# Bias and running maximum of the neighbourhood and dilated attention scores in one VectorE instruction per 128 queries

## The chip, the cores and the metric

The kernel runs on one core of one Trainium2 chip. The metric is the device time of one execution in microseconds. All tensors are fp32. A weight matrix is split into a rounded part and a rest, both in the format that TensorE multiplies fast, so each weight chunk passes through ScalarE (the rounded part, `W_hi`) and VectorE (the rest, `W_lo`) before TensorE can use it.

## The reference, cut to what matters

The model is a chain of blocks over 256 tokens of width 1024. Two of its attention stages are touched by the change: neighbourhood attention (8 heads of width 64, each query sees a window of 8 by 16 grid cells and adds a learned bias) and dilated attention (16 heads of width 64, three groups of keys at strides 1, 4 and 16, masked).

```python
# neighbourhood attention, one row of the grid
sc = einsum('bchd,bicjhd->bhcij', q_row, k_win) * dh ** -0.5
sc = sc + bias
p = softmax(sc)
return einsum('bhcij,bicjhd->bchd', p, v_win)
...
# dilated attention, one block of 128 queries, per group g of keys
sc = einsum('bqhd,bqjhd->bhqj', q_blk[:, :, g], k_sel) * dh ** -0.5
sc = where(valid, sc, -1e30)
m = max(sc); e = exp(sc - m); z = sum(e)
o = einsum('bhqj,bqjhd->bqhd', e / z, v_sel)     # groups are then merged by a softmax over m + log z
```

## The kernel before

All work of a core is written out per engine, in one fixed order, and the engines meet only in semaphores. A list of stages (`make_plan`) is walked by each engine's program. Between the attention stages lie projections and MLPs, in which TensorE streams weight chunks of 1 MB.

An attention stage (kind `attend`) goes by units. In the stages called `even` (8 neighbourhood heads `na`, then 8 latent-attention heads `mla`) and `dilated` (16 heads `dil`) a unit is a pair of heads; I call its first head a and its second head b. `even` has units 0 to 3 with `na` heads and 4 to 7 with `mla` heads; `dilated` has units 0 to 7. A head's scores lie in PSUM, as 256 queries in two halves of 128 (`t` = 0, 1) by 256 keys (`na`) or 512 keys (`dil`: 256 of stride 1, 128 each of the two others).

For each head:

- `scores(u)` on TensorE (L707) writes the scores of both heads of unit u to PSUM. It first waits until the heads that had the same banks have been read. For heads with a bias that is the semaphore `s_read`.
- `soft(n)` on VectorE adds bias or mask and finds the maximum: for `dil` one SCALAR_TENSOR_TENSOR over 128x1024 (L1211), for `na` two over 128x256 (L1219), which scale the score, add, write the sum to SBUF and raise `s_read`; then a wait for `s_read`, and one TENSOR_REDUCE (L1244) that writes the negated maximum to `e["mx"]` and raises `s_soft`.
- `exps(n)` on ScalarE (L1022) waits for `s_soft`, makes two exponentials, each with its row sum.
- `normalise(n)` on VectorE waits for both, then one RECIPROCAL (L1249) and two TENSOR_SCALAR (L1252).
- `transposes(n)` on TensorE (L725) waits for it; `keep_pt(n)` on ScalarE (L1032) copies the transposes to SBUF.
- `values(u)` on TensorE (L742, and L751 for `dil`) multiplies by the values; `output(u)` on VectorE (L1264) copies the result out.

The order within a stage is fixed by these loops. In `dilated`, TensorE goes `scores(u+1)`, `transposes` of a and b of unit u, `values(u)`; VectorE goes `normalise` a and b of u, `output(u-1)`, `soft` a and b of u+1; ScalarE goes `keep_pt` a and b of u, `exps` a and b of u+1. In `even`, scores are made two units ahead, and so is `soft`. The `soft` of the very first unit is called from within the projection in front of the stage (`open_attention`), ahead of the copy of that projection's last block (L1410 for `dilated`, L1391 for `even`); `scores` of the next unit waits for that copy. The stage behind `dilated` is the output projection `od_o`, whose first matmul is at L624.

Of the kernel before, what the change touches and what calls it, by code (L numbers as in the profile page):

```python
# [23 lines left out]
ALU = mybir.AluOpType  # L24
# [4 lines left out]
S = 256  # L29
# [5 lines left out]
EPS = 1e-6  # L35
NEG = -1e30
NA_H, NA_W = 8, 512
DIL_G, DIL_H = 3, 16
# [4 lines left out]
SLOTS = 6  # L43
# [72 lines left out]
def make_plan(w):  # L116
# [24 lines left out]
    p.add("mla_in", "mla_in")  # L141
    up("na_qk", w["ev_w_in"], 0, 1, post="copy", dest="na_qk", latents=True)
    up("na_qk", w["ev_w_in"], 256, 1, post="copy", dest="na_qk", at=512)
    p.add("mla_turn", "mla_turn")
# [54 lines left out]
def build_program(nc, a, out):  # L199
# [18 lines left out]
    with ctx:  # L218
# [109 lines left out]
        def head(what, h):  # L328
            if what == "na":
                pb = 64 * (h % 2)  # L330
                q = region(R["na_qk"] + (h // 2) * S, S)[pb:pb + 64, :]
                k = region(R["na_qk"] + (4 + h // 2) * S, S)[pb:pb + 64, :]
                v = lambda g, kt: region(R["na_v"] + kt * 512 + h * 64, 64)
                y = H0 + (h // 2) * S
                return dict(G=1, q=[q], k=[k], v=v, y_at=y, pb=pb, scale=64 ** -0.5, bias="na", R=R, h=h)
            if what == "mla":
# [6 lines left out]
            if what == "dil":  # L343
                pb, blk, pair = 64 * (h % 2), h // 8, h // 2
                q = [region(DIL0 + g * DIL_SIZE + pair * S, S)[pb:pb + 64, :] for g in range(3)]
                k = [region(DIL0 + g * DIL_SIZE + 2048 + pair * S, S)[pb:pb + 64, :] for g in range(3)]
                v = lambda g, kt: region(DIL0 + g * DIL_SIZE + 4096 + blk * 1024 + kt * 512
                                         + (h % 8) * 64, 64)
                y = H0 + pair * S
                return dict(G=3, q=q, k=k, v=v, y_at=y, pb=pb, scale=64 ** -0.5, bias="dil", R=RD, h=h)  # L350
            if what == "fox":
# [62 lines left out]
        for n, e in enumerate(heads):  # L414
# [16 lines left out]
            e["read"] = n_read  # L431
            n_read += bool(e["bias"])
            at = e["R"]["sm"]
# [147 lines left out]
        def _(pe):  # L581
# [110 lines left out]
            def scores(u):  # L692

                both = [heads[n] for n in units[u]]
                for e in both:
                    for prev in e["score_prev"]:
                        if heads[prev]["bias"]:
                            pe.wait_ge(s_read, heads[prev]["read"] + 1)
                        else:
                            pe.wait_ge(s_exp, 2 * prev + 2)  # L700
# [244 lines left out]
        def _(act):  # L945
# [14 lines left out]

            def cross(g, u, pair):

                act.wait_ge(chunk_done, g + 1)
                if not isinstance(u, int) or u >= 2:
                    act.wait_ge(acc_read, u - 1)
                A(T0[:, pair, :].rearrange("p (f t) -> p f t", f=2),  # L966
                  PS[:, 2 * pair:2 * pair + 2, S:2 * S], ACT.Copy).then_inc(cross_out, 1)

# [48 lines left out]
            def exps(n):  # L1017
                e = heads[n]
                act.wait_ge(s_soft, n + 1)
                for t in range(TT):  # L1020
                    src = e["probs"] if e["bias"] else e["scores"]
                    A(e["probs"][:, e["cols"][t]], src[:, e["cols"][t]], ACT.Exp,  # L1022
                      bias=e["mx"][:, t:t + 1], scale=1.0 if e["bias"] else e["scale"],
                      accum_out=e["z"][:, t:t + 1]).then_inc(s_exp, 1)
# [13 lines left out]
            for st in stages:  # L1038
# [17 lines left out]
                elif kind in ("up", "conv", "natural"):  # L1056
                    def body(i, ss=(0, 1)):
                        for s in ss:
# [8 lines left out]
                            if kind != "natural":  # L1067
                                cross(g0 + 2 * i + s, u0 + 2 * i + s, pairs[s])
                            if st.get("dest") == "latent" and s == 0:
# [89 lines left out]
        def _(dve):  # L1159
# [19 lines left out]
            def add_halves(st, dst, u, pair):  # L1179


                dve.wait_ge(cross_out, u - st["u"] + st["cross0"] + 1)
                return V.tensor_tensor(dst.rearrange("p (f t) -> p f t", f=2),  # L1183
                                       PS[:, 2 * pair:2 * pair + 2, 0:S],
# [12 lines left out]
            def soft(n):  # L1197
# [7 lines left out]
                if e["bias"] is None:  # L1205
# [3 lines left out]
                    return  # L1209
                if e["bias"] == "dil":  # L1210
                    V.scalar_tensor_tensor(e["probs"], e["scores"], e["scale"],  # L1211
                                           const("dil"), ALU.mult, ALU.add
                                           ).then_inc(s_read, 1)
                elif e["bias"] == "na":
                    if e["h"] == 0:
                        dve.wait_ge(bias_ready, 1)
                    for t in range(TT):
                        at = R["na_bias"] + e["h"] * SLOTS * GRID + (2 - 2 * t) * GRID
                        last = V.scalar_tensor_tensor(pr[:, t, :], sc[:, t, :], e["scale"],  # L1219
                                                      region(at, S), ALU.mult, ALU.add)  # L1220
                    last.then_inc(s_read, 1)
                else:
# [18 lines left out]
                    last.then_inc(s_soft, 1)  # L1241
                    return
                dve.wait_ge(s_read, e["read"] + 1)
                V.tensor_reduce(e["mx"], pr, AXIS.X, ALU.max, negate=True).then_inc(s_soft, 1)  # L1244

# [479 lines left out]
```

## Time and profile before

| | |
|---|---|
| median of 3 runs | 1936.98 us (1935.32 to 1937.48) |
| the profiled execution | 1936.47 us, of which the span from first to last instruction 1934.7 us |
| TensorE busy | 1848.3 us, 96% |
| VectorE busy | 1209.9 us, 63% |
| ScalarE busy | 935.0 us, 48% |
| mean granted TensorE clock | 0.987 |

The busy shares are averages over stages with different limits. The two attention stages that the change touches run from about 79 to 123 us (`even`) and from 554 to 627 us (`dilated`) after the span's start. Everything in the text below is told in us after that start.

### The profile page before, as it was taken

How to read it: one execution, taken by the hardware profiler on the slowest of the kernel's cores; microseconds unless marked ns; L12 is line 12 of the kernel's file. 1: busy time of each engine (PE TensorE's matmuls, PEld its weight loads, DVE VectorE, ACT ScalarE, POOL GpSimd, SP SyncE). 2: the span in 40 equal slices, each digit the busy share in tenths (PEclk: the TensorE clock that was granted, in tenths of full speed). 3: DMA queues.
4: the chain of work that ended last, by engine and by line, in shares of the span. 5: the costliest groups of instructions: out<-in, count | busy, mean ns of one | idle time of the engine just before them, and what ended most of it. 6: DMA issues, size and time to landing. Idle time of an engine off the chain costs nothing.

```text
span 1934.7 us, 27716 instructions
## 1 busy us (share of the span) xinstructions
PE 1848.3 (96%) x9804; PEld 1558.3 (81%) x9804; DVE 1209.9 (63%) x1436; ACT 935.0 (48%) x1384; POOL 271.9 (14%) x219
## 2 busy tenths in 40 slices
PE   8789999999997999999999999999999999989998
PEld 7668887777776888888888878888888888778886
DVE  6866655666778666466556656564646556756554
ACT  6354445333346544455545446454545445545443
POOL 2110021212200101210011940002000011020012
PEclk9899999999999999999999999999999999999999
DMA  5525654454430565555555535555535555245553
GB/s 186 178 69 162 184 194 174 173 173 154 163 120 1 173 187 191 190 161 194 192 177 190 180 131 184 185 194 182 187 110 195 179 191 185 98 141 173 177 192 130
DMA packets 214812, 319.32 MB, mean 165 GB/s; under 512 B 5984, under 2 KB 167008, under 8 KB 214496
## 3 DMA queue, kind: packets, MB, share of 16 engines
q1 hardware_dynamic: 213616, 313.45, 48.7%
q0 software_dynamic: 848, 4.85, 0.7%
q8 instruction: 37, 0.61, 0.1%
q10 hardware_dynamic: 288, 0.23, 0.0%
q14 instruction: 23, 0.19, 0.0%
HBM read 317.46 MB, written 1.05 MB: 165 GB/s over the span
## 4 chain that ended last, share of the span: by engine, by line
PE 82%; DVE 11%; issue 3%; ACT 2%; DMA 1%; POOL 1%; DVEq 0%; ACTq 0%; POOLq 0%
PE PS L619 24%; PE PS L617 12%; PE PS L624 12%; PE PS L626 12%; PE PS L625 12%; DVE W_lo L1172 5%; PE PS L613 4%; PE PS L614 2%; PE PS L707 1%; PE PS L689 1%; PE PS L725 1%; DMA W_raw<-in_mem_w_kv 1%; DVE U L1420 1%; PE PS L742 1%; ACT U L1022 0%
## 5 line engine op out<-in xcount | busy, mean ns | idle before, releaser
L1172 DVE TENSOR_TENSOR W_lo<-W_raw,W_hi 128x1024 fp32r<-128x1024 f32 x598 | 772.7, 1333 | 291.9 <-ACT W_hi L953 290.7
L619 PE MATMUL PS<-XN,W_hi 128*128 128x512 f32 x2072 | 739.5, 396 | 0.0
L953 ACT ACTIVATE W_hi<-W_raw 128x1024 fp32r<-128x1024 f32 x598 | 598.1, 1050 | 183.2 <-PE PS L626 168.6
L617 PE MATMUL PS<-XN,W_lo 128*128 128x256 f32 x2072 | 579.0, 279 | 0.0
L619 PEld LDWEIGHTS PS<-XN,W_hi 128*128 128x128 f32 x2072 | 389.2, 188 | 80.0
L617 PEld LDWEIGHTS PS<-XN,W_lo 128*128 128x128 f32 x2072 | 391.1, 189 | 13.9
L1603 POOL TENSOR_TENSOR SX<-U,SX 128x512 fp32r<-128x512 f32 (+1 forms) x98 | 128.5, 1316 | 1334.0 <-ACT SX L1015 1334.0
L624 PE MATMUL PS<-W_hi,SX 128*128 128x512 f32 x780 | 303.9, 390 | 1.4 <-issue 1.3
L626 PE MATMUL PS<-W_hi,SX 128*128 128x512 f32 x780 | 303.1, 389 | 0.0
L625 PE MATMUL PS<-W_lo,SX 128*128 128x512 f32 x780 | 303.1, 389 | 0.0
L966 ACT ACTIVATE T<-PS 128x512 f32<-128x512 f32 x152 | 90.9, 598 | 437.9 <-PE PS L619 437.9
L1183 DVE TENSOR_TENSOR T<-PS,T 128x512 f32<-128x512 f32 x128 | 88.4, 691 | 244.4 <-ACT T L966 244.4
L1015 ACT ACTIVATE SX<-U 128x512 fp32r (+2 forms) x98 | 60.5, 629 | 231.7 <-PE PS L626 231.7
L624 PEld LDWEIGHTS PS<-W_hi,SX 128*128 128x128 f32 x780 | 146.4, 188 | 32.4 <-issue 2.5
L626 PEld LDWEIGHTS PS<-W_hi,SX 128*128 128x128 f32 x780 | 146.4, 188 | 30.3
L625 PEld LDWEIGHTS PS<-W_lo,SX 128*128 128x128 f32 x780 | 146.4, 188 | 30.2
L624 PE MATMUL PS<-W_hi,XN 128*128 128x512 f32 (+2 forms) x368 | 144.4, 392 | 13.8 <-DVE W_lo L1172 13.2
L625 PE MATMUL PS<-W_lo,XN 128*128 128x512 f32 (+2 forms) x368 | 141.7, 385 | 0.0
L626 PE MATMUL PS<-W_hi,XN 128*128 128x512 f32 (+2 forms) x368 | 141.4, 384 | 0.0
L613 PE MATMUL PS<-XN,W_hi 128*128 128x512 f32 x296 | 118.8, 402 | 8.3 <-DVE W_lo L1172 7.5
L624 PEld LDWEIGHTS PS<-W_hi,XN 128*128 128x128 f32 x368 | 70.2, 191 | 32.1 <-DVE W_lo L1172 18.2
L614 PE MATMUL PS<-XN,W_lo 128*128 128x256 f32 x296 | 82.3, 278 | 0.0
(144 smaller groups left out, 1526.6 us busy)
## 6 DMA issues: line engine op xcount, KB each, us to landing
W_raw<-in_ffn_w_gate_up SPq DMA_DIRECT2D x88, 1024.0 KB, 5.1
W_raw<-in_mlp_w SPq DMA_DIRECT2D x64, 1024.0 KB, 5.2
W_raw<-in_ffn_w_down SPq DMA_DIRECT2D x44, 1024.0 KB, 4.9
W_raw<-in_od_w_in SPq DMA_DIRECT2D x36, 1024.0 KB, 4.9
W_raw<-in_a_w_in SPq DMA_DIRECT2D x14, 1024.0 KB, 5.0
W_raw<-in_mem_w_kv SPq DMA_DIRECT2D x8, 1024.0 KB, 5.2
W_raw<-in_w_kvf SPq DMA_DIRECT2D x8, 1024.0 KB, 5.4
W_raw<-in_ev_w_in SPq DMA_DIRECT2D x6, 1024.0 KB, 5.8
```

Source lines behind the costliest of these rows:

```text
L613: mm(bank, wT(W_hi, slot, k, fb), both, start=True, stop=False)
L614: mm(bank[:, S:], wT(W_lo, slot, k, fb), xn[:, k, 0, :], start=False, stop=False)
L617: mm(bank[:, S:], wT(W_lo, slot, k, fb), xn[:, k, 0, :], start=False, stop=False)
L619: last = mm(bank, wT(W_hi, slot, k, fb), both, start=False, stop=k == KD - 1)
L624: mm(bank, xh, wh, start=start, stop=False)
L625: mm(bank, xh, wl, start=False, stop=False)
L626: return mm(bank, xl, wh, start=False, stop=stop)
L953: A(W_hi[:, slot, halves(h)], W_raw[:, slot, halves(h)], ACT.Copy).then_inc(w_hi, 1)
L966: A(T0[:, pair, :].rearrange("p (f t) -> p f t", f=2), PS[:, 2 * pair:2 * pair + 2, S:2 * S], ACT.Copy).then_inc(cross_out, 1)
L1172: V.tensor_tensor(W_lo[:, slot, halves(h)], W_raw[:, slot, halves(h)], W_hi[:, slot, halves(h)], ALU.subtract).then_inc(w_lo, 1)
L1183: return V.tensor_tensor(dst.rearrange("p (f t) -> p f t", f=2), PS[:, 2 * pair:2 * pair + 2, 0:S], T0[:, pair, :].rearrange("p (f t) -> p ...
L1603: nc.gpsimd.tensor_tensor(SX[:, slot, 1, 0:st["ks"] * S], down_src(st, j), SX[:, slot, 0, 0:st["ks"] * S], ALU.subtract).then_inc(st_lo, 1)
```

## The change

`soft` for `na` and `dil` heads becomes two calls of `tensor_tensor_reduce`, one for each half of 128 queries: out = (score + bias) times a factor of `-masked`, and the running minimum of what was written, starting from 3e38, goes to `e["mx"]`. What is written is thus negated and the minimum is the negated maximum. The exponential then has a scale of -1. The instruction has only one factor, on the sum; for the masks (0 or -1e30) that factor may be the score's scale, and for the `na` bias it may not, so q is scaled by 1/8 where it leaves its projection (`times`): on ScalarE as a scale of a copy that is there already, on VectorE as SCALAR_TENSOR_TENSOR in place of TENSOR_TENSOR (2 instructions). `s_read` is no longer raised for these heads. TensorE's `scores` waits for `s_soft` of the heads that had the banks.

```diff
-    up("na_qk", w["ev_w_in"], 0, 1, post="copy", dest="na_qk", latents=True)
-    up("na_qk", w["ev_w_in"], 256, 1, post="copy", dest="na_qk", at=512)
+    up("na_qk", w["ev_w_in"], 0, 1, post="copy", dest="na_qk", latents=True, times=64 ** -0.5)
+    up("na_qk", w["ev_w_in"], 256, 1, post="copy", dest="na_qk", at=512, times=64 ** -0.5)
...
-                        if heads[prev]["bias"]:
+                        if heads[prev]["bias"] == "fox":
                             pe.wait_ge(s_read, heads[prev]["read"] + 1)
+                        elif heads[prev]["bias"]:
+                            pe.wait_ge(s_soft, prev + 1)
...
-                  PS[:, 2 * pair:2 * pair + 2, S:2 * S], ACT.Copy).then_inc(cross_out, 1)
+                  PS[:, 2 * pair:2 * pair + 2, S:2 * S], ACT.Copy, scale=times).then_inc(cross_out, 1)
...
-                      bias=e["mx"][:, t:t + 1], scale=1.0 if e["bias"] else e["scale"],
+                      bias=e["mx"][:, t:t + 1], scale={None: e["scale"], "fox": 1.0}.get(e["bias"], -1.0),
...
+                if st.get("times"):
+                    return V.scalar_tensor_tensor(dst.rearrange("p (f t) -> p f t", f=2),
+                                                  PS[:, 2 * pair:2 * pair + 2, 0:S], st["times"],
+                                                  T0[:, pair, :].rearrange("p (f t) -> p f t", f=2),
+                                                  ALU.mult, ALU.add)
...
-                if e["bias"] == "dil":
-                    V.scalar_tensor_tensor(e["probs"], e["scores"], e["scale"],
-                                           const("dil"), ALU.mult, ALU.add
-                                           ).then_inc(s_read, 1)
-                elif e["bias"] == "na":
-                    if e["h"] == 0:
+                if e["bias"] in ("na", "dil"):
+                    if (e["bias"], e["h"]) == ("na", 0):
                         dve.wait_ge(bias_ready, 1)
                     for t in range(TT):
-                        at = R["na_bias"] + e["h"] * SLOTS * GRID + (2 - 2 * t) * GRID
-                        last = V.scalar_tensor_tensor(pr[:, t, :], sc[:, t, :], e["scale"],
-                                                      region(at, S), ALU.mult, ALU.add)
-                    last.then_inc(s_read, 1)
+                        if e["bias"] == "na":
+                            add = region(R["na_bias"] + (e["h"] * SLOTS + 2 - 2 * t) * GRID, S)
+                        else:
+                            add = const("dil")[:, t * 2 * S:(t + 1) * 2 * S]
+
+                        last = V.tensor_tensor_reduce(
+                            out=pr[:, t, :], in0=sc[:, t, :], in1=add, scale=-e["masked"], scalar=FAR,
+                            op0=ALU.add, op1=ALU.min, accum_out=e["mx"][:, t:t + 1])
+                    last.then_inc(s_soft, 1)
...
-                    return
-                dve.wait_ge(s_read, e["read"] + 1)
-                V.tensor_reduce(e["mx"], pr, AXIS.X, ALU.max, negate=True).then_inc(s_soft, 1)
```

On VectorE, the turn from one unit of `dilated` to the next (the end of `normalise`, `output`, then `soft` of heads a and b) stood like this before. U, T and K are the SBUF tensors of scores and mask, ST holds the statistics.

```order
L1264 COPY U<-PS 128x4x64 [waits s_pv]
L1211 SCALAR_TENSOR_TENSOR U<-PS,K 128x1024 [waits s_pt,s_score]
L1244 TENSOR_REDUCE ST<-U 128x2 [waits s_read]
L1211 SCALAR_TENSOR_TENSOR U<-PS,K 128x1024 [waits s_pt,s_score]
L1244 TENSOR_REDUCE ST<-U 128x2 [waits s_read]
L1249 RECIPROCAL ST<-ST 128x2 [waits s_exp]
```

And after the change. Each call is emitted as two instructions: the pass over the scores, and one that writes out the running value.

```order
L1270 COPY U<-PS 128x4x64 [waits s_pv]
L1227 ISA U,ST<-PS,K 128x512 [waits s_pt,s_score]
L1227 ISA ST 128x1
L1227 ISA U,ST<-PS,K 128x512
L1227 ISA ST 128x1
L1227 ISA U,ST<-PS,K 128x512 [waits s_pt,s_score]
L1227 ISA ST 128x1
L1227 ISA U,ST<-PS,K 128x512
L1227 ISA ST 128x1
L1255 RECIPROCAL ST<-ST 128x2 [waits s_exp]
```

Four instructions became eight, of which four are of one element per partition, and the wait between sum and maximum is gone. On TensorE nothing moves; the start of `scores` in the same place waited like this before:

```order
L751 MATMUL PS<-U 64x128 x7
L707 MATMUL PS<-U 128x256 [waits s_read]
L707 MATMUL PS<-U 128x256
L707 MATMUL PS<-U 128x128 x4
L707 MATMUL PS<-U 128x256 x2
```

and waits like this after:

```order
L754 MATMUL PS<-U 64x128 x7
L710 MATMUL PS<-U 128x256 [waits s_soft]
L710 MATMUL PS<-U 128x256
L710 MATMUL PS<-U 128x128 x4
L710 MATMUL PS<-U 128x256 x2
```

The semaphore that frees the score banks is now the one raised at the end of `soft`, not the one raised when the scores had been read.

## Rows read from the trace of the kernel before

**Rows 1.** Windows of the dilated stage: length, busy of PE, PEld, DVE, ACT, POOL, PEclk
```profile
561.70:563.60 1.90, 0.01 (x2) 0.01 (x2) 1.90 (x3) 1.16 (x3) 0.00 (x0) 1.00 0.22 91
563.60:566.10 2.50, 2.50 (x24) 2.16 (x24) 1.84 (x6) 0.36 (x2) 0.00 (x0) 0.75 0.00 0
...
617.00:619.80 2.80, 0.02 (x1) 0.02 (x1) 2.65 (x5) 1.93 (x7) 0.00 (x0) 0.94 0.00 0
619.80:627.00 7.20, 7.00 (x41) 5.35 (x41) 1.57 (x4) 5.66 (x10) 2.75 (x2) 0.55 0.00 0
```

**Rows 2.** Timeline of one dilated unit: start, duration, engine, line, operation, [idle before <-releaser]
```profile
582.26 1.23 DVE L1211 SCALAR_TENSOR_TENSOR T<-PS,K 128x1024 f32<-128x1024 f32 x1
...
584.67 1.21 DVE L1211 SCALAR_TENSOR_TENSOR T<-PS,K 128x1024 f32<-128x1024 f32 x1
585.92 1.22 DVE L1244 TENSOR_REDUCE ST<-T 128x2 f32<-128x1024 f32 x1
...
586.14 2.03 PE L707 MATMUL PS<-U 64*128 64x256 f32 x24 [0.79 <-DVE T L1211]
...
587.17 0.72 ACT L1022 ACTIVATE T<-T,ST 128x512 f32<-128x512 f32 x1 [0.86 <-DVE ST L1244]
...
588.72 0.17 DVE L1249 RECIPROCAL ST<-ST 128x2 f32<-128x2 f32 x1 [0.60 <-ACT T L1022]
...
590.18 1.22 DVE L1211 SCALAR_TENSOR_TENSOR U<-PS,K 128x1024 f32<-128x1024 f32 x1
```

**Rows 3.** Timeline of TensorE from the dilated stage's third `scores` to its fourth
```profile
571.44 2.03 PE L707 MATMUL PS<-U 64*128 64x256 f32 x24
...
574.83 1.07 PE L725 MATMUL PS<-K,T 128*128 128x128 f32 x8 [0.34 <-ACT U L1032]
...
576.23 1.08 PE L742 MATMUL PS<-U 128*64 128x256 f32 x8 [0.34 <-ACT U L1032]
...
578.24 2.03 PE L707 MATMUL PS<-U 64*128 64x256 f32 x24
```

**Rows 4.** Timeline at the dilated stage's opening and end
```profile
562.32 1.21 DVE L1410 COPY U<-PS 128x1024 f32<-128x1024 f32 x1
...
563.59 2.61 PE L707 MATMUL PS<-U 64*128 64x256 f32 x24 [1.92 <-DVE U L1410]
...
620.10 0.19 ACT L1022 ACTIVATION_READ_ACCUMULATOR T<-T,ST 128x1 f32 x1
...
626.91 0.50 PE L624 MATMUL PS<-W_hi,SX 128*128 128x512 f32 x1
```

**Rows 5.** Groups of VectorE by form: count, busy us, mean ns of one, idle before
```profile
L1219 DVE SCALAR_TENSOR_TENSOR U<-PS,U 128x256 f32<-128x256 f32 x16 | 6.0, 415 | 2.0 <-PE PS L707 2.0
L1234 DVE SCALAR_TENSOR_TENSOR U<-U,ST,K 128x256 f32<-128x256 f32 x8 | 3.8, 479 | 0.0
```

**Rows 6.** Timeline of VectorE at the first `mla` unit of `even`
```profile
103.09 0.68 DVE L1206 TENSOR_REDUCE ST<-PS 128x2 f32<-128x512 f32 x1
...
103.81 0.17 DVE L1207 TENSOR_SCALAR ST<-ST 128x2 f32<-128x2 f32 x1
103.89 0.69 DVE L1206 TENSOR_REDUCE ST<-PS 128x2 f32<-128x512 f32 x1
```

**Rows 7.** Timeline of the `na` units of `even`, `soft` of unit 1 first
```profile
85.21 0.75 DVE L1219 SCALAR_TENSOR_TENSOR U<-PS,U 128x256 f32<-128x256 f32 x2
...
88.93 1.94 PE L725 MATMUL PS<-K,U 128*128 128x128 f32 x8 [4.90 <-DVE U L1252]
...
92.93 0.76 DVE L1219 SCALAR_TENSOR_TENSOR U<-PS,U 128x256 f32<-128x256 f32 x2 [1.97 <-PE PS L707]
...
95.82 0.51 ACT L1022 ACTIVATE U<-U,ST 128x256 f32<-128x256 f32 x1 [0.29 <-DVE ST L1244]
...
98.01 0.74 DVE L1219 SCALAR_TENSOR_TENSOR U<-PS,U 128x256 f32<-128x256 f32 x2
```

**Rows 8.** Window at the end of `even`, columns as in rows 1
```profile
117.10:118.90 1.80, 0.00 (x0) 0.03 (x1) 1.67 (x6) 1.80 (x7) 0.00 (x0) 1.00 0.00 0
```

More of the change, by code:

```diff
@@ L36 @@
 NEG = -1e30
+FAR = 3e38
 NA_H, NA_W = 8, 512
@@ L334, in head @@
                 y = H0 + (h // 2) * S
-                return dict(G=1, q=[q], k=[k], v=v, y_at=y, pb=pb, scale=64 ** -0.5, bias="na", R=R, h=h)
+                return dict(G=1, q=[q], k=[k], v=v, y_at=y, pb=pb, scale=64 ** -0.5, masked=1.0, bias="na", R=R, h=h)
             if what == "mla":
@@ L349, in head @@
                 y = H0 + pair * S
-                return dict(G=3, q=q, k=k, v=v, y_at=y, pb=pb, scale=64 ** -0.5, bias="dil", R=RD, h=h)
+                return dict(G=3, q=q, k=k, v=v, y_at=y, pb=pb, scale=64 ** -0.5, masked=64 ** -0.5, bias="dil", R=RD, h=h)
             if what == "fox":
@@ L431, in build_program @@
             e["read"] = n_read
-            n_read += bool(e["bias"])
+            n_read += e["bias"] == "fox"
             at = e["R"]["sm"]
@@ L959, in ahead, with cross @@
                     split_hi(g + 1, 1 - slot)
-            def cross(g, u, pair):
+            def cross(g, u, pair, times=1.0):
                 act.wait_ge(chunk_done, g + 1)
@@ L1067, in body @@
                             if kind != "natural":
-                                cross(g0 + 2 * i + s, u0 + 2 * i + s, pairs[s])
+                                cross(g0 + 2 * i + s, u0 + 2 * i + s, pairs[s], st.get("times", 1.0))
                             if st.get("dest") == "latent" and s == 0:
```

## The prediction

> **What bounds the kernel now.** TensorE is busy 96% of the span, but that is an average over stages, so I went to the places where the changed lines run. The busy groups of VectorE say where: L1211, L1219 and their L1244 run only in `even` (about 79 to 123) and `dilated` (554 to 627). I then read the chain of waits there, the timeline to see what each engine waits for, and last the granted clock.
>
> In `dilated` the middle units are a ring through VectorE and ScalarE [rows 2]. `soft` of head a starts at 582.26, that of head b at 584.67, its maximum at 585.92, and the exponentials of b can start at 587.17: 4.9 us of `soft`. They take 1.55 (587.17 to 588.72, where RECIPROCAL had waited 0.60 for them). From there, normalising b and the copy of the output take 1.46 to the next `soft` at 590.18. Sum 7.92, and that is the period: 590.18 - 582.26. TensorE waits in it: its `scores` at 586.14 had been idle 0.79 for head b's sum (L1211).
>
> TensorE has a shorter ring of its own. From the third `scores` to the fourth, 571.44 to 578.24, it takes 6.80 [rows 3]: transposes of b start 3.39 in, `values` 1.40 later, and two short waits of 0.34 for ScalarE's copies are part of it. So a unit costs 7.9 where VectorE sets the pace and 6.8 where TensorE does, and the trace of before has one of each kind.
>
> Both ends of the stage wait for VectorE too. At the opening, the copy L1410 starts at 562.32, behind `soft`, though TensorE has stood still since 561.67 (it starts at 563.59 after 1.92 idle) [rows 4]. TensorE's clock, still 1.00 while it stands, is 0.75 in the next 2.5 us [rows 1]. At the end TensorE does next to nothing for 2.8 us, and the 7.2 after it run at 0.55, close to the lower level of 1.2 GHz [rows 1].
>
> In `even` the `na` units have the same ring: 92.93 to 98.01 is 5.08, the next, to 103.09, again 5.08 [rows 6, 7]. `soft` takes 2.89 until b's exponentials start at 95.82, and 2.19 follow. In front of the first transposes at 88.93 TensorE had been idle 4.90, and what released it was VectorE's normalisation, which stands behind `soft` of unit 1 from 85.21 on.
>
> **The price of the new instruction.** The trace has none of its kind. A head of `dil` now takes two passes of 128x512 and two short instructions that write out one value; I call pass and write-out together c, and c' for the 128x256 of `na`. Lower bound: an instruction over 128x512 takes 0.69, one over two values 0.17, and the next one starts 0.08 after such a short one's start [rows 6], so the last 0.08 or so of each lie under its successor. That is 0.61 + 0.08 = 0.69 for c. A 128x256 takes 0.415 [rows 5], two of them 0.75 [rows 7]: 0.34 + 0.08 = 0.42 for c'. Upper bound for a pass at the ordinary rate: nothing overlaps, 0.69 + 0.17 = 0.86 and 0.415 + 0.17 = 0.59. I take 0.75 and 0.46, nearer to the lower ends, since the short instruction in rows 6 overlaps on both sides. `soft` of both heads is then 4c = 3.0 instead of 4.9 in `dilated`, and 4c' = 1.84 instead of 2.8 in `even`.
>
> The Trainium skill (Vector Engine (DVE) Microarchitecture Reference, Measured stream behaviour on trn2) gives built-in operations and programs of several micro-operations alike 1.04 ns per column and some 75 ns per instruction. By that page c would be an estimated 0.68; the sum would stay the same, as will be seen, since 6.8 is then set by TensorE.
>
> **Even, -2.5.** The first `soft` pair (at 81) lies under TensorE's projection: nothing. That of unit 1 is in front of the first transposes: 88.93 comes 0.9 earlier (2.77 of `soft` to 1.84). The two rings behind it become 0.05 + 2c' (head a) + 1.13 (a's exponentials) + 2.19 = 4.3, since b's exponentials now wait for a's and not for b's maximum: 0.8 less each. The `mla` units are unchanged. 0.9 + 1.6 = 2.5.
>
> **Dilated, opening, -0.6.** `soft` of unit 0 from 557.55 on now ends at about 560.6. The copy L1410 starts when the last chunk is done, 561.7, lasts 1.21, and TensorE starts at 563.0 instead of 563.59.
>
> **First unit, -1.0.** From 563.59 to 571.44 are 7.85, of which a part is the fallen clock. TensorE's idle time in front becomes 1.3 us instead of 1.92. I take the clock as staying up, as it does at the end of `even`, where TensorE stands still for 1.8 us at 1.00 [rows 8]. The unit then costs 6.8.
>
> **Middle units, -4.5.** The unit of rows 3 stays. The four behind it cost 7.92 each and become 6.8. The other rings must be shorter than 6.8 for that. Through VectorE: 4c + 1.55 + 1.46 = 6.0 (0.1 more if a's exponentials hold b's up). Across two units: `scores` waits now for `s_soft`, so `soft` (4c), 0.25 to `scores`, 3.4 to transposes b, 1.9 to ScalarE's second copy, 3.1 for both heads' exponentials, 1.46: 4c + 10.1 = 13.1 for two, 6.55 for one. So the new wait costs nothing while c is under 0.87. The upper bound of c lies just there: that is why its price hardly matters.
>
> **Last unit, -3.6.** From the last `scores` to the end of b's exponentials are 10.5 now (586.14 to 588.72 + 7.92). In the new order ScalarE has finished its copies 3.4 + 1.9 = 5.3 after that `scores` and does both heads' exponentials in 3.1: 8.4, a gain of 2.1. From the end of the exponentials (620.29) to `od_o` at 626.91 are 6.6 [rows 4]. In this piece transposes b and `values` take about 5 at the low clock and 3.41 at the full one (574.83 to 578.24). TensorE's idle time in front of transposes a falls from 2.8 to about 1.2, so I take the full clock: 1.5 less.
>
> Behind the stage, the weight chunks are loaded and split in an order that hangs on TensorE's progress and moves with it.
>
> **The other edits, 0.** The scale on ScalarE's copies is a parameter of an instruction that is there. The two SCALAR_TENSOR_TENSOR over 128x512 replace instructions of the same size (0.69).
>
> **Sum.** 2.5 + 0.6 + 1.0 + 4.5 + 3.6 = 12.2. The profiled execution took 1936.5 (span 1934.7 and 1.8 around it), which gives 1924.3; the median of the runs lies 0.5 above the profiled one: 1924.8. VectorE's busy time falls by some 19 us, of which 12 are on the path.
>
> **The rivals.**
> (1) The clock falls anyway at one or both ends: gain 12.2 less 1.0 and/or 1.5, 1926 to 1927.3. For it: the clock fell behind 1.92 us of idle TensorE and stayed up behind 1.8, which are close together, and the work in front differed. Chance 0.23.
> (2) The instruction is dearer by a fixed part, c about 1.0 and c' 0.7, for instance because the write-out waits for the pass to drain and for something to be set up. Then the two-unit ring is 7.05, `even` gains nothing, and about 7.5 remain: 1929.5. Nothing in the trace shows such a part; nothing excludes it. 0.13.
> (3) The gain is nil: the pass goes at two clocks per element, because it reads two tensors, writes one and keeps a running value. c = 2 x 0.53 + 0.15 = 1.22 or so, c' = 0.69: `soft` takes as long as before in both stages, all rings stay. Time 1937. SCALAR_TENSOR_TENSOR from PSUM (0.415) and with both inputs in SBUF (0.479) [rows 5] go at about one clock, so a second stream alone doesn't do it. 0.09.
> The Trainium skill (Vector Engine (DVE) Microarchitecture Reference, Points that are easy to get wrong) says that the scalar-tensor-tensor layout halves its throughput with two SBUF sources that are not bf16, since no read port is left for the accumulator. Here one source is PSUM, and L1234's 0.479 contradicts a halving for the form without accumulator; by that page's rule, extended to PSUM, it would be this rival.
> (4) Slower: the same half rate with the write-out not overlapped, c from 1.32. Each 0.1 above 1.22 adds 0.4 to seven `soft` pairs in `dilated` and to three in `even`, 4 us in all, so 1.32 is where it becomes measurably slower; at 1.38 (nothing overlapped) 1943. `scores` would then also wait 1.9 longer for `s_soft` than for `s_read`, hidden behind the VectorE ring of 8.6. 0.03.
>
> **How the numbers follow.** Forecast with the clock up 0.50, rival 1 0.23, rival 2 0.13, rival 3 0.09, rival 4 0.03, and 0.02 for more gain (TensorE's ring under 6.8). A measurement of this kernel can tell about 0.2%, 3.9 us, from no change. Faster by over that: 0.50 + 0.23 + 0.02 + most of rival 2, 0.87. Same: rival 3 and the dear end of 2, 0.10. Slower 0.03. Range: below, the lower bounds of c and c' and 0.5 of spread, 1922; above, to the middle of rival 2 and a little more, 1932.
>
> **What would show it.** In the changed trace: passes of 0.69 and 0.42 with starts 0.7 to 0.85 and 0.42 to 0.6 apart; L1416, the copy at the opening, released by TensorE and not by `soft`; periods of 6.8 in `dilated` with TensorE hardly waiting for VectorE, 4.3 in the `na` units; clock 1.00 in both ends. Wrong would be: c over 0.87, seen as `scores` waiting for the write-out (L1227); periods of 7.9; the clock at 0.55 behind the last exponentials.

## The result, and the profile after

The changed kernel takes 1921.01 us (median of 4 runs, 1919.76 to 1922.01), the kernel before 1936.48 us beside it (4 runs, 1935.32 to 1937.48): ratio 0.992, interval 0.9903 to 0.9937. That is 15.5 us less where 12.2 were forecast, and 1 us below the lower end of the range. Direction and mechanism held; sizes were too small, and so was the margin below. I take them here in the order of the sum.

The groups of VectorE by form (count, busy us, mean ns of one) give the new instruction its price.

```profile
L1227 DVE CUSTOM_DVE_ANT_0 T<-PS,K 128x512 f32<-128x512 f32 x16 | 10.1, 688 | 0.1
L1227 DVE CUSTOM_DVE_ANT_0 U<-PS,K 128x512 f32<-128x512 f32 x16 | 10.1, 684 | 0.0
...
L1227 DVE CUSTOM_DVE_ANT_0 U<-PS,U 128x256 f32<-128x256 f32 x16 | 5.8, 419 | 1.7 <-PE PS L710 1.7
...
L1227 DVE DVE_READ_ACCUMULATOR2_ANT ST<- 128x1 f32 x48 | 4.0, 83 | 0.0
```

A pass costs what the instructions of its size in [rows 5, 6] cost (0.69 and 0.42 us); the write-out has a row of its own, 0.083 us. What counts on the path is the distance of the starts. The timeline of a `dilated` unit, VectorE's rows (start, duration; it answers to [rows 2]):

```profile
582.07 0.68 DVE L1227 CUSTOM_DVE_ANT_0 U<-PS,K 128x512 f32<-128x512 f32 x1
582.68 0.08 DVE L1227 DVE_READ_ACCUMULATOR2_ANT ST<- 128x1 f32 x1
582.68 0.69 DVE L1227 CUSTOM_DVE_ANT_0 U<-PS,K 128x512 f32<-128x512 f32 x1
583.29 0.09 DVE L1227 DVE_READ_ACCUMULATOR2_ANT ST<- 128x1 f32 x1
583.29 0.69 DVE L1227 CUSTOM_DVE_ANT_0 U<-PS,K 128x512 f32<-128x512 f32 x1
...
583.90 0.69 DVE L1227 CUSTOM_DVE_ANT_0 U<-PS,K 128x512 f32<-128x512 f32 x1
584.51 0.09 DVE L1227 DVE_READ_ACCUMULATOR2_ANT ST<- 128x1 f32 x1
585.90 0.17 DVE L1255 RECIPROCAL ST<-ST 128x2 f32<-128x2 f32 x1 [1.30 <-ACT U L1025]
...
588.75 0.69 DVE L1227 CUSTOM_DVE_ANT_0 T<-PS,K 128x512 f32<-128x512 f32 x1
```

The write-out and the next pass start at the same moment (582.68, 583.29). So c is 0.61, not 0.75: the write-out costs nothing. `soft` of both heads lasts 2.53 us to the end of its last write-out (2.44 to its start) where it lasted 4.9, and VectorE now waits 1.30 for ScalarE's exponentials. The unit takes 588.75 - 582.07 = 6.68.

The Trainium skill (Vector Engine (DVE) Microarchitecture Reference, Measured stream behaviour on trn2) gives some 75 ns per instruction and 1.04 per column, by which I estimate 608 ns for 512 columns and 342 for 256. The trace agrees with that for the distance from one pass to the next (0.61 and, below, 0.34 to 0.35), if the write-out is counted as nothing.

TensorE in the same stage (it answers to [rows 3]) and at the stage's ends (to [rows 4]). The stage's very first `scores`, that of unit 0, is made within the projection in front (550.26); from here on "the first `scores`" is the one that opens the stage, that of unit 1. First the timeline of TensorE from there on:

```profile
559.27 2.02 PE L710 MATMUL PS<-U 64*128 64x256 f32 x24 [1.32 <-DVE U L1416]
...
565.96 2.03 PE L710 MATMUL PS<-U 64*128 64x256 f32 x24
...
572.64 2.02 PE L710 MATMUL PS<-U 64*128 64x256 f32 x24
...
599.38 2.02 PE L710 MATMUL PS<-U 64*128 64x256 f32 x24
...
607.09 1.09 PE L728 MATMUL PS<-K,T 128*128 128x128 f32 x8 [0.96 <-DVE T L1258]
...
612.28 0.50 PE L625 MATMUL PS<-W_hi,SX 128*128 128x512 f32 x1
```

Every unit takes 6.68, the first too, and no `scores` behind the first waits for VectorE. The copy L1416 started at 557.99, released by TensorE and not behind `soft` any more; TensorE's idle time in front of the first `scores` is 1.32 instead of 1.92. The windows at both ends (length; busy PE, PEld, DVE, ACT, POOL; granted clock; as in [rows 1]):

```profile
559.30:561.80 2.50, 2.50 (x29) 2.29 (x30) 2.30 (x6) 0.00 (x0) 0.00 (x0) 1.00 0.00 0
604.60:607.10 2.50, 1.54 (x24) 1.19 (x19) 1.10 (x5) 2.50 (x7) 0.00 (x0) 1.00 0.02 7
607.10:612.20 5.10, 3.95 (x40) 3.27 (x40) 1.58 (x4) 4.78 (x10) 2.75 (x2) 1.00 0.00 0
```

The clock is 1.00 at both, where it was 0.75 and 0.55. In `even` (it answers to [rows 7]) TensorE's first transposes come at 87.55, not 88.93, and the `na` rings behind it are 95.29 - 91.31 = 3.98 and 3.98 again to the first `mla` maximum:

```profile
87.55 1.94 PE L728 MATMUL PS<-K,U 128*128 128x128 f32 x8 [3.51 <-DVE U L1258]
...
91.31 0.42 DVE L1227 CUSTOM_DVE_ANT_0 U<-PS,U 128x256 f32<-128x256 f32 x1 [1.72 <-PE PS L710]
...
91.66 0.42 DVE L1227 CUSTOM_DVE_ANT_0 U<-PS,U 128x256 f32<-128x256 f32 x1
...
92.12 0.51 ACT L1025 ACTIVATE U<-U,ST 128x256 f32<-128x256 f32 x1 [1.99 <-DVE ST L1227]
...
93.12 0.49 ACT L1025 ACTIVATE U<-U,ST 128x256 f32<-128x256 f32 x1
...
95.29 0.41 DVE L1227 CUSTOM_DVE_ANT_0 U<-PS,U 128x256 f32<-128x256 f32 x1
...
99.27 0.68 DVE L1214 TENSOR_REDUCE ST<-PS 128x2 f32<-128x512 f32 x1
```

**Where the time went.** In the two profiled executions (1936.5 and 1919.8) `even` gives 3.8: 1.4 in front of the transposes, 0.2 from there to the next `soft` (a matter of the clock, see below), 1.1 for each ring. `dilated` gives 0.6 at the opening and 10.3 from the first `scores` to `od_o` (612.28 - 559.27 = 53.01, before 626.91 - 563.59 = 63.32). That makes 14.7 of 16.7. The other 2.0 lie behind `dilated`, most of it at one place: a matmul of a later stage that reads its input from the SBUF tensor XM. The kernel before, first timeline, then windows:

```profile
843.43 0.50 PE L613 MATMUL PS<-XM,W_hi 128*128 128x512 f32 x1 [1.81 <-DVE W_lo L1172]
```
```profile
844.00:846.00 2.00, 2.00 (x11) 1.72 (x10) 1.04 (x2) 0.34 (x1) 1.50 (x3) 0.69 0.64 167
846.00:848.00 2.00, 2.00 (x7) 1.68 (x7) 2.00 (x3) 0.00 (x0) 0.00 (x0) 0.50 1.01 352
```

And the changed kernel at the same place of the program:

```profile
828.80 0.50 PE L614 MATMUL PS<-XM,W_hi 128*128 128x512 f32 x1 [1.83 <-DVE W_lo L1175]
```
```profile
828.80:832.80 4.00, 4.00 (x23) 3.48 (x24) 3.01 (x4) 0.91 (x1) 1.99 (x4) 1.00 0.68 226
```

The same matmul, the same idle time in front of it, and the clock falls to its lower level for 3.4 us in the one and stays up in the other. The experiments return to this.

### The profile page after: what moved, and what is told of

It reads as the page before. It is cut to its first block, busy times and chain, and to the rows that moved or that the text cites. A ratio compares the mean times of both kernels' runs of the same rounds, so it can differ in the third digit from the quotient of the medians.

```text
span 1918.0 us, 27756 instructions
## 1 busy us (share of the span) xinstructions
PE 1839.3 (96%) x9804; PEld 1551.4 (81%) x9804; DVE 1187.4 (62%) x1476; ACT 932.5 (49%) x1384; POOL 272.6 (14%) x219
## 3 DMA queue, kind: packets, MB, share of 16 engines
q0 software_dynamic: 848, 4.85, 0.7%
## 4 chain that ended last, share of the span: by engine, by line
PE 85%; DVE 10%; ACT 3%; issue 2%; POOL 1%; DMA 0%; DVEq 0%; ACTq 0%; POOLq 0%
PE PS L620 24%; PE PS L625 13%; PE PS L627 12%; PE PS L626 12%; PE PS L618 12%; DVE W_lo L1175 4%; PE PS L614 4%; PE PS L615 2%; PE PS L710 1%; PE PS L690 1%; PE PS L728 1%; PE PS L745 1%; ACT U L1035 1%; DVE U L1426 1%; ACT U L1025 1%
```

## The experiments

The theory after the result: all of the gain comes from the shorter `soft` in the two stages; in `dilated` it is bounded by TensorE's own ring of 6.68, and the clock at the two ends is a part of it. Rivals: the scaling of q or the exponential's new factor matter; the gain is mostly clock; VectorE still sets the pace. All kernels below that are timed stand beside runs of the kernel before on the same chip.

### One stage alone, and q's scale alone

`only_na` has the new `soft`, the scaled q and the new wait for `na` heads, and the old lines for `dil`; `only_dil` is the reverse. `only_q_scale` is the kernel before with the scale of q moved, and nothing else:

```diff
-    up("na_qk", w["ev_w_in"], 0, 1, post="copy", dest="na_qk", latents=True)
+    up("na_qk", w["ev_w_in"], 0, 1, post="copy", dest="na_qk", latents=True, times=64 ** -0.5)
...
-                return dict(G=1, q=[q], k=[k], v=v, y_at=y, pb=pb, scale=64 ** -0.5, bias="na", R=R, h=h)
+                return dict(G=1, q=[q], k=[k], v=v, y_at=y, pb=pb, scale=1.0, bias="na", R=R, h=h)
```

> Only the neighbourhood heads (and the scale of q that they need) are changed; the dilated heads are as before. Theory A (the gain is the shortened soft in two rings, and the parts add): the changed kernel's trace has the even stage 3.8 us shorter, so this one takes 1936.5 - 3.8 = 1932.7, na period 3.98, dilated periods 7.9. Rival B (much of the gain of the whole change comes from elsewhere, by the clock, once anything moves): 1934 or more, or 1930 and less, with clock falls appearing or vanishing outside the two stages.

> Only the dilated heads are changed; the neighbourhood heads are as before. Theory A: 1936.5 - 10.9 = 1925.6; even period 5.08, dilated period 6.68, clock 1.00 at both ends of the dilated stage. Rival B: this kernel alone reaches nearly the whole gain (1922), since what is over 14.7 us in the whole change came with any shift behind the even stage.

> The kernel before, with q scaled where it leaves its projection (scale on two ScalarE copies, two SCALAR_TENSOR_TENSOR in place of TENSOR_TENSOR), and the old two-step soft with a factor of 1. Theory A: no change, 1936.5 within 1 us. Rival: the two edits cost or give up to 0.5 us each, seen between 25 and 60 us in the trace.

| | median us, runs | before beside it | ratio, interval |
|---|---|---|---|
| `only_na` | 1932.74, 10 | 1935.98, 26 | 0.9981, 0.997 to 0.9992 |
| `only_dil` | 1926.18, 5 | the same | 0.9942, 0.9929 to 0.9956 |
| `only_q_scale` | 1936.95, 10 | the same | 1.000, 0.999 to 1.0009 |

The two halves of the change add up: by the ratios 0.19% and 0.58%, that is 3.7 us (interval 1.5 to 5.8) and 11.2 (8.5 to 13.7), together 14.9; by the medians 3.2 and 9.8, together 13.0. The stages in the trace gave 3.8 and 10.9. The scale of q costs nothing. In `only_na` the `dilated` stage behaves as before, down to the clock falls at both ends. TensorE's timeline there, and the windows at the opening and behind the last exponentials:

```profile
559.16 3.24 PE L710 MATMUL PS<-U 64*128 64x256 f32 x24 [1.92 <-DVE U L1423]
...
582.11 2.02 PE L710 MATMUL PS<-U 64*128 64x256 f32 x24 [0.78 <-DVE T L1219]
...
590.01 2.02 PE L710 MATMUL PS<-U 64*128 64x256 f32 x24 [0.78 <-DVE U L1219]
```
```profile
559.10:561.60 2.50, 2.44 (x20) 2.24 (x22) 1.91 (x7) 0.43 (x2) 0.00 (x0) 0.63 0.00 0
...
615.70:622.40 6.70, 5.57 (x41) 4.21 (x41) 1.57 (x4) 5.65 (x10) 2.75 (x2) 0.75 0.00 0
```

### The clock alone

`warm_ends` is the kernel before with 6 matmuls more in TensorE's wait at the opening of `dilated` and 9 more in front of the last unit's transposes; nothing reads their results.

```diff
+                    if st["name"] == "dilated":
+                        for _ in range(6):
+                            mm(PS[:, 2 * (u0 % 2), :], XN[:, 0, 0, 0:P], both_halves(XN, 0),
+                               start=True, stop=True)
...
+                        if st["name"] == "dilated" and u == us[-1]:
+                            pe.wait_ge(h_done, e_out_done(units[u - 2][-1]))
+                            for _ in range(9):
+                                mm(PS[:, 2 + u % 2, :], XN[:, 0, 0, 0:P], both_halves(XN, 0),
+                                   start=True, stop=True)
```

> The kernel before, with matmuls whose result nobody reads: six while TensorE waits for the copy at the opening of the dilated stage, nine while it waits for the last unit's normalisation. They keep TensorE busy and delay nothing that it waits for. Theory A (of the 10.9 us in the dilated stage, what lies in the first and the last unit is for a good part the granted clock): the clock stays at 1.00 in both places, the first unit goes from 7.85 to about 6.8 or 7, the end from 17.1 to about 15.4: 2.7 us less in all, 1933.8. Rival C (the ends gained by VectorE's time alone, the clock falls anyway): 1936.5, clock 0.5 to 0.7 in both places as before.

Measured: 1934.17 (11 runs) against 1935.98, ratio 0.9988, interval 0.9978 to 0.9997. The windows of its opening and its end:

```profile
563.30:565.80 2.50, 2.50 (x29) 2.29 (x30) 2.29 (x6) 0.35 (x2) 0.00 (x0) 1.00 0.00 0
...
618.60:624.00 5.40, 3.92 (x40) 3.28 (x40) 1.58 (x5) 5.07 (x10) 2.75 (x2) 1.00 0.00 0
```

The clock stays up at both ends, and from the first `scores` to `od_o` the stage takes 60.84 instead of 63.32. The first unit gives 1.17, the next takes 0.35 of it back (7.15 instead of 6.80: VectorE's ring catches up), the last gives 1.68. So the clock is worth 2.5 us in the kernel before. In the changed kernel nothing takes the 0.35 back, and its two parts make 2.8 of the 10.3. The gain is therefore not mostly clock. The median is 1.8 lower than that of the kernel before, by the ratio 2.3, with an interval from 0.6 to 4.3; 2.7 were expected.

### How far VectorE is from setting the pace

The changed kernel with 1, 2 or 4 more VectorE instructions per `dil` head, each a maximum over 128x256 whose result nothing uses, in front of the second pass:

```diff
+                        if e["bias"] == "dil" and t == 1:
+                            for i in range(4):
+                                at = 40 + 8 * (e["unit"] % 2) + 4 * e["slot"] + i
+                                V.tensor_reduce(ST[:, at:at + 1], sc[:, t, 0:S], AXIS.X, ALU.max)
```

> The changed kernel with one extra TENSOR_REDUCE over 128x256 of PSUM in each dilated head's soft (its result is not used): 0.34 us more of VectorE per head, soft of a pair 3.1 instead of 2.44. Theory A (TensorE's ring of 6.68 is the limit, VectorE's rings are shorter): the period stays 6.68. Rival (VectorE's ring still sets the pace, 6.68 is just where it came out): 7.36.

> As pad1 with two such instructions per head: soft of a pair 3.8. Theory A: VectorE's ring, soft + 3.04 = 6.84, now just passes TensorE's, and the ring over two units, (soft + 9.6) / 2, is 6.70; so the period is 6.84. Rival: 8.0 (every us of soft counts from 2.44 on).

> As pad1 with four such instructions per head: soft of a pair 5.16, more than the 4.9 of the kernel before. Theory A: soft + 3.04 = 8.2 per unit, so a half-rate instruction (soft 4.9) would have given nothing. A rival by which the late s_soft costs TensorE more than the late s_read did (scores begin only behind the whole soft): above 8.6.

| from the first `scores` to `od_o` | stage us | period of the middle units |
|---|---|---|
| changed kernel, `only_dil`, `halves` | 53.01 each | 6.68 |
| `pad1` | 53.01 | 6.68 |
| `pad2` | 54.26 | 6.85 to 6.93 |
| `pad4` | 64.46 | 8.21 |
| kernel before | 63.32 | 7.90 |

One run each, 1920.93, 1922.94 and 1933.69 us, so the traces decide here and not the times. 0.33 us more per head are hidden entirely, 0.66 show by 0.2 per unit, 1.33 bring back a ring through VectorE (the 64.46 also hold two clock falls, at the opening, behind 2.24 us of idle time, and at the end). VectorE's timeline of `pad4`:

```profile
589.67 0.68 DVE L1231 CUSTOM_DVE_ANT_0 U<-PS,K 128x512 f32<-128x512 f32 x1
590.28 0.09 DVE L1231 DVE_READ_ACCUMULATOR2_ANT ST<- 128x1 f32 x1
590.28 1.42 DVE L1230 TENSOR_REDUCE ST<-PS 128x1 f32<-128x256 f32 x4
591.61 0.68 DVE L1231 CUSTOM_DVE_ANT_0 U<-PS,K 128x512 f32<-128x512 f32 x1
...
594.96 0.88 DVE L1262 TENSOR_SCALAR U<-U,ST 128x512 f32<-128x512 f32 x2
```

`soft` of both heads lasts 5.1 there (589.67 to 594.76), as it would about with an instruction at half rate (4 times 1.22 is 4.9). The prediction's rival of no gain is thereby right about what half rate would do in this stage. It also settles the new wait: in `pad4` each `scores` stands idle 1.46 until `soft` ends and waits for it by name, and the period, 8.21, is that of the ring through VectorE (5.1 and 3.0 make 8.1), as the prediction had it.

### TensorE's order in a unit

If TensorE's ring is the bound, its waits of 0.34 for ScalarE's copies might be filled: `reorder` puts the `scores` of the next unit between the transposes of a and of b, from the second unit on.

```diff
-                        if st["name"] == "dilated" and u + 1 in us:
+                        late = st["name"] == "dilated" and u != us[0]
+                        if st["name"] == "dilated" and u + 1 in us and not late:
                             scores(u + 1)
                         for n_ in units[u]:
                             transposes(n_)
+                            if late and n_ == units[u][0] and u + 1 in us:
+                                scores(u + 1)
```

> The changed kernel with scores(u+1) of the dilated stage issued between the transposes of head a and head b, except in the first unit. TensorE's ring has two waits of 0.34 for ScalarE's copies. Theory A: the one in front of transposes b is filled by the scores, the period falls from 6.68 to 6.34, six units, 2 us less than the changed kernel. Rival D: soft starts 1.1 later and its ring becomes the limit, or ScalarE's copies of a and b bunch up: period 6.68 or longer.

Measured: 1925.75 (5 runs, 1923.85 to 1926.08) against 1936.16 (9 runs), ratio 0.9944, interval 0.9931 to 0.9958. The stage took 56.87, 3.9 more than the changed kernel's, and the period was 7.33, not 6.34. The expectation failed. The timeline of one unit of `reorder`:

```profile
574.97 2.03 PE L710 MATMUL PS<-U 64*128 64x256 f32 x24
...
577.04 0.69 DVE L1230 CUSTOM_DVE_ANT_0 T<-PS,K 128x512 f32<-128x512 f32 x1 [1.21 <-PE PS L710]
...
578.58 0.72 ACT L1028 ACTIVATE T<-T,ST 128x512 f32<-128x512 f32 x1
...
580.13 0.17 DVE L1258 RECIPROCAL ST<-ST 128x2 f32<-128x2 f32 x1 [0.56 <-ACT T L1028]
...
581.27 1.09 PE L728 MATMUL PS<-K,T 128*128 128x128 f32 x8 [0.96 <-DVE T L1261]
```

I had counted the work of TensorE and not what the move makes of the loop. `scores` (574.97) releases `soft` at 577.04, that the exponentials (578.58), these RECIPROCAL (580.13) and the normalisation, that the transposes of a (581.27), and behind these stands the next `scores`, at 582.29. 2.07 + 1.54 + 1.55 + 1.14 + 1.02 = 7.32: one unit's whole chain now lies in one period. In the old order the transposes of a stand behind the next unit's `scores`, so the chain up to them, 6.30 here, had a whole period and those 2 us more: in the changed kernel they start 581.28 - 572.64 = 8.64 behind their `scores`. Rival D (6.68 or longer, since `soft` starts later) was right.

### `s_soft` raised per half, and both together

`halves` raises `s_soft` behind each pass of 128 queries, so that the exponential of the first half need not wait for the second; `both_better` has that and `reorder`; `changed_again` is the changed kernel once more, on the same chip.

```diff
-                act.wait_ge(s_soft, n + 1)
+                    act.wait_ge(s_soft, 2 * n + (t + 1 if e["bias"] in ("na", "dil") else 2))
...
-                            op0=ALU.add, op1=ALU.min, accum_out=e["mx"][:, t:t + 1])
-                    last.then_inc(s_soft, 1)
+                            op0=ALU.add, op1=ALU.min, accum_out=e["mx"][:, t:t + 1]).then_inc(s_soft, 1)
```

> The changed kernel with s_soft raised for each half of 128 queries, so that the first exponential of a head starts behind the first pass and not behind the second. Theory A: the na period is first pass 0.34 + gap 0.12 + four exponentials 2.0 + 1.06 = 3.6 instead of 3.98, twice; the dilated units stay at 6.68, since ScalarE is held there by its copies; 0.8 us less than the changed kernel in all. Rival: TensorE holds the na units at 3.95, as it does the mla units, and nothing is gained.

> reorder and halves together. Theory A: the gains add, 2.8 us less than the changed kernel; 0 if neither helps.

> The changed kernel again, on one chip with the two below. The two stages give 14.7 us by the trace. Theory E (the rest of the measured 15.5, and of the 16.7 between the two profiled executions, is where the clock happens to fall elsewhere in an execution): the difference of the medians lies between 14 and 16, single runs of either kernel scatter in steps of about 1.7 us, and the clock's falls outside the two stages differ between executions of the same kernel. Rival F (the change removes a clock fall at about 845 us, behind the dilated stage, each time): 16 to 16.7.

| | median us, 5 runs each | ratio to before (1935.83, 9 runs) |
|---|---|---|
| `changed_again` | 1922.38 | 0.9932, 0.9918 to 0.9946 |
| `halves` | 1920.34 | 0.9924, 0.991 to 0.9937 |
| `both_better` | 1926.75 | 0.995, 0.9937 to 0.9964 |

`halves` shortens the part that it should. Its timeline of `even`:

```profile
91.63 0.42 DVE L1227 CUSTOM_DVE_ANT_0 U<-PS,U 128x256 f32<-128x256 f32 x1 [1.78 <-PE PS L710]
...
92.10 0.51 ACT L1025 ACTIVATE U<-U,ST 128x256 f32<-128x256 f32 x1 [1.75 <-DVE ST L1227]
...
95.27 0.41 DVE L1227 CUSTOM_DVE_ANT_0 U<-PS,U 128x256 f32<-128x256 f32 x1
...
99.06 0.69 DVE L1214 TENSOR_REDUCE ST<-PS 128x2 f32<-128x512 f32 x1
```

The exponentials start 0.47 behind `soft`'s start instead of 0.81, and the two rings are 3.64 and 3.79 instead of 3.98. The second ring is held by TensorE, as the rival had it: its `scores` (97.13, 1.89 long) are not ready sooner, and the maximum at 99.06 starts 0.49 behind the copy in front of it instead of 0.33. That is 0.5 us instead of the expected 0.8, and the `mla` units give it back: they take 4.02 to 4.39 where the changed kernel has 3.95, and from the maximum at 99.06 to the stage's last output copy are 20.6 us instead of 19.9. What holds them up was not tested. In `dilated`, where TensorE sets the pace, it gives nothing (53.01). The medians of `halves` and `changed_again` are 2.0 apart, but the intervals overlap, and none of it can be laid to the edit. `both_better` fails with `reorder`: its period is 7.33 too, and it is slower than the changed kernel by 4.4 where it was to be 2.8 faster. The changed kernel's gain, repeated, is 13.5 us by the medians (interval of the ratio 10.5 to 15.9), just under the 14 to 16 that were expected; the 14.7 of the two stages lie between 13.5 and 15.5.

The repeat also shows what in the first trace was the execution's and not the change's. `changed_again`, the timeline of `even` and a window of it:

```profile
86.79 1.94 PE L728 MATMUL PS<-K,U 128*128 128x128 f32 x8 [3.51 <-DVE U L1258]
...
90.79 0.42 DVE L1227 CUSTOM_DVE_ANT_0 U<-PS,U 128x256 f32<-128x256 f32 x1 [1.97 <-PE PS L710]
```
```profile
90.70:92.40 1.70, 1.70 (x10) 0.74 (x8) 1.47 (x8) 0.80 (x3) 0.00 (x0) 0.50 0.00 0
```

The same kernel, the same 3.51 of idle time in front of the transposes; but here the next `soft` starts 4.00 behind them, as in the kernel before, and not 3.76, because TensorE's clock is still at 0.50 where it was back at 1.00 in the first trace. The first ring is then 4.09 instead of 3.98, and `even` gives 3.5 instead of 3.8. `dilated` takes 53.01 in both.

### The fall of the clock behind `dilated`

In the profiled executions the clock falls behind the same XM matmul in the kernel before, `only_na`, `only_q_scale`, `reorder` and `both_better`, and not in the changed kernel, `changed_again`, `halves`, `only_dil`, the three padded kernels and `warm_ends`. `reorder` for example, with the new `soft`:

```profile
833.00:835.00 2.00, 2.00 (x10) 1.71 (x9) 1.17 (x2) 0.18 (x1) 1.40 (x2) 0.67 0.72 225
835.00:837.00 2.00, 2.00 (x7) 1.61 (x7) 2.00 (x3) 0.00 (x0) 0.00 (x0) 0.50 0.86 300
```

It goes neither with the instruction (`reorder` has the new `soft` and the fall, `warm_ends` neither) nor with the stage's length (`pad4` and `reorder` are on the wrong sides). Other falls come and go between executions of one kernel, as `even` in the two traces of the changed kernel shows. Its four runs stand in two pairs, 1919.76 and 1920.17 with a mean clock of 0.993, 1921.86 and 1922.01 with 0.991. Whether the 1.6 us of this fall belong to the change stays open.

## What of the prediction held, and which steps failed

- **What bounds the kernel.** Held: VectorE's ring set the pace in both stages, and TensorE's ring took its place in `dilated`. In `even` the ring through VectorE and ScalarE remained, shorter.
- **The price of the instruction.** Mis-sized. I took 0.75 and 0.46, and even the lower bounds (0.69 and 0.42) were too high: measured 0.61 and 0.345. The step that failed here is the one in which pass and write-out each keep a start distance of their own, 0.08 for the short one, as in [rows 6]. There the short instruction reads its predecessor's result and starts behind its end, 0.72 after its start; the write-out starts 0.61 behind its pass, together with its successor. In `dilated` this cost the forecast nothing, since TensorE sets the pace there; in `even` it makes 0.9 of the difference.
- **Even, -2.5.** Measured 3.8, in the repeat 3.5. In front of the transposes 1.4 instead of 0.9, and each ring 1.1 instead of 0.8, mostly from c' (4 and 2 times 0.115), the rest from b's exponentials, which follow a's without a gap. The last 0.2 are luck: the transposes and `scores` behind the idle time run at the lower clock level in both kernels, and in this execution it rose early, 91.31 - 87.55 = 3.76 against 92.93 - 88.93 = 4.00 before. Of the nine traces with the new `soft` in `even` and the same 3.51 of idle time, three have 3.76 to 3.81, six, `changed_again` among them, 3.99 or 4.00.
- **Opening, -0.6.** Held.
- **First unit, -1.0.** 1.16. The clock stayed up, which was taken and not known; `warm_ends`, which keeps the clock up with matmuls that nobody reads and leaves `soft` as it was, gives it 1.17. The ground on which it was taken was weak: at the end of `even`, where [rows 8] has 1.00, the clock fell to 0.50 in `pad4`, whose `even` stage is that of the changed kernel, behind the same 1.84 us of idle time.
- **The unit of rows 3 stays; four units, -4.5.** Measured 0.12 and 4.85. One error in both: 6.80 was not TensorE's own ring. From transposes of b to `values` it takes the same 1.40 as before, but from `values` to the next `scores` 1.89, and in [rows 3] 2.01: that `scores` had itself waited 0.12 for head b's sum. Own ring 6.68.
- **Last unit, -3.6.** 4.18. The exponentials end 7.98 behind the last `scores` instead of 8.4, since ScalarE starts them at 5.0 and not 5.3 and takes 2.96 for the four; the clock part is 1.68, not 1.5.
- **The other edits, 0.** Held (`only_q_scale`).
- **Sum.** 14.7 in the two stages against 12.2: 1.3 of the difference in `even`, 1.2 in `dilated`. Against the median it is 15.5, interval 12.2 to 18.8; the 0.8 on top lie within it. No single term missed by much; the steps that failed are the price c' (0.46 where 0.345 was measured, 0.9 of the difference), TensorE's ring (6.80 where it is 6.68, some 0.6) and the exponentials of the last unit (0.4). The lower end of the range failed too. Redone with c' at 0.42 and 0.5 of spread it is 1924.0, since c has no part in `dilated`; the other 2 us down to 1922 had no term, and clock falls elsewhere, which the two pairs of runs above put at some 2, were not in it. The repeat's 1922.4 lies just inside, the first measurement just outside.
- **The rivals.** (1) the clock falls anyway: no, 1.00 at both ends. (2) and (3), a dearer or slower instruction: no, 0.61. `pad4` shows that a `soft` as long as before would have left the ring through VectorE in place. The half rate that the Trainium skill names for two SBUF sources (Vector Engine (DVE) Microarchitecture Reference, Points that are easy to get wrong) isn't seen with one source in PSUM: 0.61 for 512 columns; two SBUF sources were not tried with this instruction. (4): no.

## What to carry to other kernels

Where a VectorE sum and a maximum over the same scores stand in a ring, fusing them is worth its time only until the next engine's ring; measure that ring at a place where nobody is waited for, down to the tenth, since a wait of 0.12 can hide in it. Before moving work forward on an engine, add up the whole chain that then has to fit in one period: an engine's own sum of work is not its ring. VectorE's write-out behind a pass cost nothing here and need not be charged. For each idle stretch of TensorE that the change shortens, give the clock a term with a chance of its own, and repeat the trace before you explain a few tenths by it: the same idle time went with and without a fall here.

## What the runs showed of the hardware

- The write-out of VectorE's running value takes 0.083 us. In 37 of 48 places the next instruction follows at once; there both start together, and the write-out delays it by nothing, also where that is the RECIPROCAL behind the last one in `even` (both at 86.59). The Trainium skill (VectorE: DVE Perf Modes, Two Vector instructions with no wait between them) says that an op that writes out its accumulator is two instructions; the trace agrees, 48 and 48. ScalarE's row sum has a start distance of its own: in the last `dilated` unit its read starts 0.62 behind the exponential and the next exponential 0.09 behind the read (604.40, 605.02, 605.11).
- TensorE's clock at the opening of `dilated` sorted with the idle time in front: behind 1.92 us of it (kernel before, `only_na`, `only_q_scale`) and 2.24 (`pad4`) it fell, behind 1.32 (the changed kernel and the seven others that have the new opening) it did not. At the XM matmul behind `dilated`, 1.81 to 1.83 us of idle time went with a fall in five traces and with none in eight; at the end of `even`, 1.84 went with a fall in `pad4` and with none in the kernel before and the changed kernel.
